# First products of 32 more expert chunks between the gate groups of a fused two-layer kernel

## The chip, the cores and the metric

The kernel runs on one core of one Trainium2 chip. The metric is the device time of one execution in microseconds. Lower is better. Before the change three timed runs gave 1766.4, 1764.07 and 1761.23 us, median 1764.07.

## The reference, cut to what matters

Two transformer layers follow each other on 256 tokens of width 1024, all in float32. The change touches two places of the first layer: the merge of its two branches, and the mixture of experts behind it.

```python
merged = sigmoid(ga) * (y_a @ w_branch_a) + sigmoid(gb) * (y_b @ w_branch_b)
h = h + merged @ w_out
n2 = rmsnorm(h, norm2_g)
# peer: 8 heads, 128 x 128 = 16384 experts, 16 chosen for each head and token
s1, s2 = scores of n2 @ wq against two sets of 128 keys
v1, i1 = top_k(s1, 16); v2, i2 = top_k(s2, 16)
vals, ci = top_k(v1[:, None] + v2[None, :], 16)     # of 256 candidates
idx = i1[ci // 16] * 128 + i2[ci % 16]; gates = softmax(vals)
h = expert_u[idx] . n2                              # the first products
out = sum(gelu(h) * gates * expert_v[idx])          # the second products
```

## The kernel before, in words

The kernel does not gather experts. It computes all 16384 of them for all 256 tokens, as 128 chunks of 128 experts, and multiplies gelu(h) by a dense gate matrix G (for each chunk, 128 experts by 256 tokens) that is zero where an expert was not chosen. Each float32 product is made of three faster ones: a weight part is split into a rounded high part (whi, written by ScalarE) and the rest (wlo, written by VectorE, or by GpSimd as bfloat16 where `pooled` says so), and so are the activations.

Weights stream from HBM in items of 1 MiB into `raw`, a ring of three slots; the SyncE queue issues them in order, each when the rest of the second part of the item three before has been written. An item is two parts of 1024 columns, one for each product of a chunk; whi and wlo are rings of three parts (`NBUF`).

The stages around the change, in order on TensorE:

1. Merge. `wide_panel` makes pa and pb (the two branch products, four banks each). VectorE multiplies them by the gates (L1707), GpSimd adds the two branches (L581), TensorE transposes the sum (L648), ScalarE and VectorE write it as high and low parts (L1195, L1591), and the output projection follows.
2. Queries and choice. TensorE computes queries and scores of 8 heads. VectorE picks the 16 best of each head (L1725 to L1748) and works out indices and gates (L1755 to L1780). Beside it TensorE computes the first products of the first `EARLY` = 24 chunks with `u_part` (24 matmuls of 256 columns; L659), ScalarE writes gelu(h) into G (L1255), and GpSimd writes the wlo of these parts (L491), up to part S_PRE - 1.
3. Gates. When `sel_ready` is set, indices and gates are transposed, and G is built in 32 groups of 8 tokens. For a group VectorE writes two one-hot matrices (L1803, 6 and 8 tokens) and two scaled ones (L1813), ScalarE scales six (L1284), TensorE multiplies them (`gate_products`, L904; 8 products, 16 records), ScalarE copies the gates of the chunks from EARLY on into G (`gate_copy`, L1291), and VectorE multiplies the gates into the first EARLY chunks, which hold gelu(h) already (`gate_times`, L1797). One-hots live in idle ring buffers, two groups deep.
4. Second products of the early chunks (`output`, `v_part`: 12 matmuls of 512 columns; L659), with one part of weights for each chunk.
5. The other 104 chunks: for each, `u_wide` (8 matmuls of 512 and 8 of 256 columns; L694, L696) two chunks ahead, then `v_part`. VectorE sums, multiplies by the gate and splits (L1851 to L1862).

The order of work on each engine is the order of the program text; engines meet at semaphores, and a wait holds up all that stands behind it on its engine.

Of the kernel before, what the change touches and what calls it, by code (L numbers as in the profile page):

```python
# [19 lines left out]
BY_ACT = 6  # L20
NEG = -3.0e38
# [24 lines left out]
EARLY = 24  # L46
# [69 lines left out]
def _wide(name, count):  # L116
    for _ in range(count - 1):
        _part()
    _part(main=f"{name}3")
    _use(*[(f"{name}{i}", "dve") for i in range(4)])  # L120
# [3 lines left out]
_wide("pb", 4)  # L124
# [13 lines left out]
assert _parts == S_LATE and EARLY % UN == 0 and (P - 2 - EARLY) % UN == 0  # L138
# [38 lines left out]


T_PART = {"n1": -1, "ya": S_WA - 1, "yb": S_WA + 3, "mg": S_WO - 1, "n2": S_WQ - 1, "idx": S_PRE - 1,
# [26 lines left out]
def program(nc, x, panels1, experts, ffa, panels2, ffb, cols, conv_cols, w_low, w_gate_up, w_sgu, k12, w_dt,  # L206
# [9 lines left out]
    with ctx:  # L216
# [50 lines left out]
        QP_AT = 24000  # L267
# [11 lines left out]
        QP = cut(16, T)  # L279
        MDEC, WG, ALR = cut(P), cut(512), cut(T)  # L280
# [13 lines left out]
        CAND = cut(NT, PEER_H, 256)  # L294
        PICK = cut(TOPK * NT * P // 2).bitcast(bf16).rearrange("p (j n) -> p j n", j=TOPK)
        VAL = cut(NT, 16, TOPK)
        IDF = cut(NT, 16, TOPK)
        BEST = cut(NT, P)
# [3 lines left out]
        IDX = cut(NT, 16, TOPK).bitcast(u32)  # L302
        CI = cut(NT, P).bitcast(u32)
        CIA = cut(NT, P).bitcast(u32)
        PST = cut(NT, PEER_H)
        assert cut.at <= QP_AT
# [75 lines left out]
        hot_ready, one_ready, one_scaled = sem("hot_ready"), sem("one_ready"), sem("one_scaled")  # L382
        gate_mm, gate_out, gate_mul = sem("gate_mm"), sem("gate_out"), sem("gate_mul")
# [69 lines left out]
        def half(item, h):  # L453
            return raw[:, item % RING, PART * h:PART * h + PART]
# [10 lines left out]
        def round_part(act, p):  # L465

            act.wait_ge(slot_ready[item_of(p) % RING], 16 * (item_of(p) // RING + 1))
            if p >= NBUF:
                wait_part_used(act, p - NBUF)
            act.activation(whi[:, p % NBUF, :], half(item_of(p), p % 2), ACT.Copy).then_inc(part_hi, 1)  # L470

        def pooled(p):

            return S_WQ <= p < S_PRE or S_ZZ <= p < S_WM
# [1730 lines left out]
```

## Time and profile before

| | |
|---|---|
| median of three timed runs | 1764.07 us |
| profiled execution, device time | 1760.97 us |
| its span, first to last instruction | 1759.3 us |
| mean granted TensorE clock | 0.959 |
| TensorE busy (matmul) | 1605.1 us, 91% |
| VectorE busy | 1254.6 us, 71% |
| ScalarE busy | 798.4 us, 45% |
| GpSimd busy | 145.2 us, 8% |

Busy times are sums over the whole span and say nothing of a single stage. A granted clock of 1.00 is 2.4 GHz and one of 0.50 is 1.2 GHz. Matmuls are pipelined: the record of one is longer than its share, so a run of them is measured from start to start.

### The profile page before, as it was taken

To read this page: it belongs to the slowest core of one execution; us is meant where nothing else is said; L and a number is where in the kernel's file an instruction comes from. 1 tells how busy PE (TensorE), PEld (TensorE's weight loads), DVE (VectorE), ACT (ScalarE), POOL (GpSimd) and SP (SyncE) were. 2 spreads that over 40 slices of the span, in tenths; PEclk is the share of its full clock that TensorE was granted. 3 is DMA by queue.
4 is the path that set the end of the run, shared out by engine and by line. 5 is a ranking of instruction groups with operands and counts; after the bars stand their busy time and mean duration, and the time that the engine had idled before them with its cause. 6 is when DMAs were issued, how large, how long until landed. Compare 5 with 4: busy or idle time off the path is not lost.

```text
span 1759.3 us, 25517 instructions
## 1 busy us (share of the span) xinstructions
PE 1605.1 (91%) x8766; PEld 1361.4 (77%) x8766; DVE 1254.6 (71%) x2098; ACT 798.4 (45%) x1190; POOL 145.2 (8%) x86
## 2 busy tenths in 40 slices
PE   6999799857899999999999999799979886879997
PEld 5777588756778888888888888688869856568886
DVE  4575469999767777777777777677774695567776
ACT  4544345469534444444444444544443533244443
POOL 1000267600000000000000000000000062000000
PEclk9999899989999999999999999899998997889999
DMA  5534334400345555555555555455543340235552
GB/s 191 186 140 154 143 122 167 143 1 0 142 169 184 189 186 186 189 190 189 191 191 191 191 191 201 138 191 191 186 160 108 108 144 1 89 139 191 191 191 95
DMA packets 38949, 270.34 MB, mean 154 GB/s; under 512 B 4706, under 2 KB 5218, under 8 KB 6643
## 3 DMA queue, kind: packets, MB, share of 16 engines
q1 hardware_dynamic: 37296, 266.97, 42.6%
q10 hardware_dynamic: 1602, 2.71, 0.5%
q8 instruction: 30, 0.49, 0.1%
q14 instruction: 21, 0.16, 0.0%
HBM read 268.62 MB, written 1.05 MB: 153 GB/s over the span
## 4 chain that ended last, share of the span: by engine, by line
PE 75%; DVE 17%; ACT 3%; issue 2%; DVEq 1%; DMA 1%; POOL 0%; SPq 0%; ACTq 0%
PE ps L659 38%; PE ps L694 20%; PE ps L696 9%; PE ps L648 2%; DVE wlo L1803 2%; PE ps L693 1%; DVE arena L2047 1%; DVE wlo L491 1%; DVE arena L2028 1%; DVE arena L1748 1%; PE ps L766 1%; DVE arena L1728 1%; DVE arena L1731 1%; DVE arena L1737 1%; ACT whi L470 1%
## 5 line engine op out<-in xcount | busy, mean ns | idle before, releaser
L694 PE MATMUL ps<-XT,whi 128*128 128x512 f32 x1536 | 554.1, 399 | 1.9 <-DVE wlo L491 1.9
L696 PE MATMUL ps<-XT,wlo 128*128 128x256 f32 x1344 | 378.6, 282 | 0.0
L694 PEld LDWEIGHTS ps<-XT,whi 128*128 128x128 f32 x1536 | 287.5, 189 | 60.6 <-DVE wlo L491 2.2
L470 ACT ACTIVATE whi<-raw 128x1024 fp32r<-128x1024 f32 x170 | 178.9, 1058 | 229.5 <-PE ps L659 177.2
L659 PE MATMUL ps<-whi,HAh 128*128 128x512 f32 x688 | 270.1, 393 | 4.8 <-DVE HAl L1926 2.3
L659 PE MATMUL ps<-wlo,HAh 128*128 128x512 f32 x688 | 269.0, 391 | 0.0
L659 PE MATMUL ps<-whi,HAl 128*128 128x512 f32 x688 | 268.3, 390 | 0.0
L696 PEld LDWEIGHTS ps<-XT,wlo 128*128 128x128 f32 x1344 | 255.6, 190 | 7.5
L491 DVE TENSOR_TENSOR wlo<-raw,whi 128x1024 fp32r<-128x1024 f32 x134 | 162.8, 1223 | 116.7 <-ACT whi L470 115.3
L1875 DVE TENSOR_TENSOR wlo<-raw,whi 128x1024 fp32r<-128x1024 f32 x192 | 232.5, 1221 | 2.0
L659 PE MATMUL ps<-XT,whi 128*128 128x256 f32 x1024 | 193.1, 314 | 4.8 <-DVE wlo L491 4.8
L1372 ACT ACTIVATE whi<-raw 128x1024 fp32r<-128x1024 f32 x108 | 114.6, 1061 | 175.3 <-PE ps L694 114.3
L659 PE MATMUL ps<-whi,XT 128*128 128x512 f32 x576 | 183.4, 406 | 11.4 <-DVE wlo L491 4.4
L1943 DVE TENSOR_TENSOR wlo<-raw,whi 128x1024 fp32r<-128x1024 f32 x108 | 132.2, 1224 | 70.7 <-ACT whi L1372 69.5
L1327 ACT ACTIVATE whi<-raw 128x1024 fp32r<-128x1024 f32 x96 | 101.9, 1061 | 165.0 <-PE ps L694 165.0
L659 PEld LDWEIGHTS ps<-XT,whi 128*128 128x128 f32 x1024 | 165.4, 201 | 6.4 <-issue 4.6
L1325 ACT ACTIVATE whi<-raw 128x1024 fp32r<-128x1024 f32 x96 | 102.1, 1064 | 134.8 <-PE ps L659 134.8
L659 PEld LDWEIGHTS ps<-wlo,HAh 128*128 128x128 f32 x688 | 129.5, 188 | 28.6
L659 PEld LDWEIGHTS ps<-whi,HAh 128*128 128x128 f32 x688 | 130.0, 189 | 27.6 <-issue 6.1
L659 PEld LDWEIGHTS ps<-whi,HAl 128*128 128x128 f32 x688 | 129.7, 188 | 28.0
L491 POOL TENSOR_TENSOR arena<-raw,whi 128x1024 bf16<-128x1024 f32 x48 | 116.4, 2427 | 371.1 <-ACT whi L470 364.8
L659 PEld LDWEIGHTS ps<-whi,XT 128*128 128x128 f32 x576 | 108.6, 191 | 34.8 <-DVE wlo L491 5.9
(264 smaller groups left out, 1985.7 us busy)
## 6 DMA issues: line engine op xcount, KB each, us to landing
raw<-in_experts SPq DMA_DIRECT2D x128, 1024.0 KB, 4.8
raw<-in_panels SPq DMA_DIRECT2D x58, 1024.0 KB, 4.8
raw<-in_ffa SPq DMA_DIRECT2D x33, 1024.0 KB, 4.8
raw<-in_ffb SPq DMA_DIRECT2D x33, 1024.0 KB, 4.8
arena<-in_row_post ACTq DMA_DIRECT2D x3, 512.0 KB, 3.7
X<-in_x SPq DMA_DIRECT2D x2, 512.0 KB, 5.7
out<-X SPq DMA_DIRECT2D x2, 512.0 KB, 2.7
arena<-in_row_ln ACTq DMA_DIRECT2D x2, 256.0 KB, 7.8
```

What stands on the lines that cost most here:

```text
L470: act.activation(whi[:, p % NBUF, :], half(item_of(p), p % 2), ACT.Copy).then_inc(part_hi, 1)
L491: eng.tensor_tensor(low_weights(p), half(item_of(p), p % 2), whi[:, p % NBUF, :].bitcast(f32), ALU.subtract).then_inc(part_lo, 1)
L648: last = pe.transpose(t_bank(stage, j)[:, P * q:P * q + P], s, ident[:, :])
L659: last = pe.matmul(out, x if w_moving else w, w if w_moving else x, start=start and n == 0, stop=stop and n == 2)
L694: last = pe.matmul(out, wh[:, k], XT[:, k], start=k == 0, stop=k == NK - 1)
L696: pe.matmul(out[:, T:], wl[:, k], XTh[:, k], start=False, stop=False)
L1325: act.activation(whi[:, p % NBUF, :], half(item_of(p), 0), ACT.Copy).then_inc(part_hi, 1)
L1327: act.activation(whi[:, (p + 1) % NBUF, :], half(item_of(p), 1), ACT.Copy).then_inc(part_hi, 1)
L1372: act.activation(whi[:, q % NBUF, :], half(item_of(q), q % 2), ACT.Copy)\
L1803: return dve.tensor_tensor(out, iota.bitcast(f32).unsqueeze(1).broadcast_to(shape), idx[:, bass.ds(g * ONES, n)].unsqueeze(2).broadcast_to ...
L1875: dve.tensor_tensor(wlo[:, (p + j) % NBUF, :], half(item_of(p), j), whi[:, (p + j) % NBUF, :].bitcast(f32), ALU.subtract).then_inc(part_lo, 1)
L1943: dve.tensor_tensor(wlo[:, q % NBUF, :], half(item_of(q), q % 2), whi[:, q % NBUF, :].bitcast(f32), ALU.subtract).then_inc(part_lo, 1)
```

## The change

`EARLY` becomes `FIRST + BESIDE` = 28 + 32 = 60. The first products of 28 chunks stand where those of 24 stood. Those of 32 more are computed between the gate groups, one chunk with `u_part` ahead of each group's products. For each group ScalarE also applies gelu to this chunk in PSUM and rounds the next weight part; VectorE also writes the rest of a weight part, multiplies the gates of 60 chunks instead of 24 and then multiplies gelu(h) into the chunk's slot of G (`beside_times`). GpSimd sets these 32 slots to 1.0 beforehand, in one memset. While groups run, raw, whi and wlo are rings of two; the third slot of each holds the one-hots. 60 chunks then go through stage 4, and 68 are left for stage 5.

In the merge, pb is finished in the order of column halves, VectorE makes the four additions that GpSimd made, and the transposes of the first half wait for the first two of them only. The tail of the choice on VectorE also changes its order: the copy of iota and the rest of part S_G stand ahead of the softmax instead of behind it. GpSimd writes the rests up to part S_G - 1, four more than before.

```diff
-EARLY = 24
+FIRST, BESIDE = 28, 32
+EARLY = FIRST + BESIDE
+S_G = S_EXP + FIRST
...
+BY_HALF = (0, 2, 1, 3)
 _wide("pa", 4)
-_wide("pb", 4)
+_wide("pb", 4, BY_HALF)
...
+I_G, I_PRE = EXP0 + FIRST // 2, EXP0 + EARLY // 2
+def ring_of(n, turn, two, three):
+    if n < two:
+        return n % turn
+    if n < three:
+        return (two + (n - two) % 2) % turn
+    return (two + (n - three)) % turn
+PART_BUF = [ring_of(p, NBUF, S_G, S_PRE) for p in range(S_END)]
+ITEM_SLOT = [ring_of(i, RING, I_G, I_PRE) for i in range(ITEMS)]
+SPARE_BUF, SPARE_SLOT = (S_G + 2) % NBUF, (I_G + 2) % RING
...
-        ones_item = EXP0 + EARLY // 2 + 2
-        ones_slot = ones_item % RING
-        b1 = (S_PRE + 1) % NBUF
-        ONE1 = whi[:, b1:b1 + 2].rearrange("p b (j c) -> p b j c", j=ONES)
-        HOT2 = wlo[:, b1:b1 + 2].rearrange("p b (j c) -> p b j c", j=ONES)
-        ONE2 = raw[:, ones_slot].rearrange("p (b j c) -> p b j c", b=2, j=ONES)
+        ONE1 = [t[:, SPARE_BUF].rearrange("p (j c) -> p j c", j=ONES) for t in (whi, wlo)]
+        ONE2 = raw[:, SPARE_SLOT].rearrange("p (b j c) -> p b j c", b=2, j=ONES)
...
-            return S_WQ <= p < S_PRE or S_ZZ <= p < S_WM
+            return S_WQ <= p < S_G or S_ZZ <= p < S_WM
...
-            stream(EXP0, EARLY // 2, experts, S_EXP)
-            stream(EXP0 + EARLY // 2, P - EARLY // 2, experts[EARLY // 2:], S_PRE)
+            stream(EXP0, FIRST // 2, experts, S_EXP)
+            beside = experts[FIRST // 2:]
+            for j in range(2):
+                load(I_G + j, beside[j])
+            with sp.Fori(0, BESIDE // 4 - 1, 1) as i:
+                for s in range(2):
+                    slot = ITEM_SLOT[I_G + s]
+                    sp.wait_ge(part_lo, i * 4 + (S_G + 2 * s + 2))
+                    sp.dma_start(raw[:, slot, :], beside[i * 2 + (2 + s)]).then_inc(slot_ready[slot], 16)
+            stream(I_PRE, P - EARLY // 2, experts[EARLY // 2:], S_PRE)
...
-            for i in range(4):
-                tt, c = i // 2, slice(512 * (i % 2), 512 * (i % 2) + 512)
-                read_out(pool, f"pb{i}")
-                pool.tensor_tensor(XN[:, tt, c], GA[:, tt, c], GB[:, tt, c], ALU.add).then_inc(merged, 1)
+            pool.wait_ge(merged, 4)
+            pool.memset(G[:, FIRST:EARLY, :], 1.0).then_inc(beside_ones, 1)
             pool.wait_ge(part_lo, S_WQ)
-            for p in range(S_WQ, S_PRE):
+            for p in range(S_WQ, S_G):
...
-            wide_panel(pb, S_WB, range(4, 8))
-            pe.wait_ge(merged, 4)
-            transposes("mg", tiles(XN, NK))
+            wide_panel(pb, S_WB, range(4, 8), order=BY_HALF)
+            transposes("mg", tiles(XN, NK), by_half=merged)
...
-                                     ONE1[:, b, j, :].bitcast(f32), ONE2[:, b, j, :], start=True, stop=True)
+                                     ONE1[b][:, j, :].bitcast(f32), ONE2[:, b, j, :], start=True, stop=True)
                 last.then_inc(gate_mm, 1)
-            pe.wait_ge(gelu_done, EARLY)
-            for g in range(2):
+            def beside(g, s):
+                pe.wait_ge(part_lo, g + (S_G + 1))
+                pe.wait_ge(beside_done, g - 1)
+                u_part(ps[:, s % 2, 0:T], S_G + s).then_inc(h_done, 1)
                 pe.wait_ge(one_ready, g + 1)
                 pe.wait_ge(one_scaled, g + 1)
-                gate_products(g)
-            with pe.Fori(1, T // (2 * ONES), 1) as pair:
-                g = pair * 2
-                for b in range(2):
-                    pe.wait_ge(one_ready, g + (b + 1))
-                    pe.wait_ge(one_scaled, g + (b + 1))
-                    pe.wait_ge(gate_out, g + (b - 1))
-                    pe.wait_ge(gate_mul, g + (b - 1))
-                    gate_products(b)
+                pe.wait_ge(gate_out, g - 1)
+                pe.wait_ge(gate_mul, g - 1)
+                gate_products(s % 2)
+            pe.wait_ge(gelu_done, FIRST)
+            for g in range(FOUR):
+                if g < 2:
+                    pe.wait_ge(part_lo, S_G + g + 1)
+                    u_part(ps[:, g, 0:T], S_G + g).then_inc(h_done, 1)
+                    pe.wait_ge(one_ready, g + 1)
+                    pe.wait_ge(one_scaled, g + 1)
+                    gate_products(g)
+                else:
+                    beside(g, g)
+            with pe.Fori(1, BESIDE // FOUR, 1) as i:
+                for s in range(FOUR):
+                    beside(i * FOUR + s, s)
             pe.wait_ge(gate_out, T // ONES)
             pe.wait_ge(gate_mul, T // ONES)
+            pe.wait_ge(beside_done, BESIDE)
...
+            def beside_gelu(g, b):
+                act.wait_ge(h_done, g + (FIRST + 1))
+                act.activation(ps[:, b, 0:T], ps[:, b, 0:T], ACT.Gelu_apprx_tanh).then_inc(gelu_done, 1)
             gate_scale(0, 0)
-            gate_scale(1, 1)
-            gate_copy(0, 0)
-            with act.Fori(1, T // (2 * ONES), 1) as pair:
-                g = pair * 2
-                for b in range(2):
-                    gate_scale(g + b, b)
-                    gate_copy(g + (b - 1), 1 - b)
-            gate_copy(T // ONES - 1, 1)
+            split_to(S_G + 1)
+            for g in range(1, FOUR):
+                beside_gelu(g - 1, (g - 1) % 2)
+                split_to(S_G + g + 1)
+                gate_copy(g - 1, (g - 1) % 2)
+                gate_scale(g, g % 2)
+            with act.Fori(1, BESIDE // FOUR, 1) as i:
+                for s in range(FOUR):
+                    g, p = i * FOUR + s, S_G + s + 1
+                    beside_gelu(g - 1, (s - 1) % 2)
+                    wait_loaded(act, item_of(p), i * 16)
+                    act.wait_ge(h_done, g + FIRST)
+                    act.activation(whi[:, buf(p), :], half(item_of(p), p % 2), ACT.Copy).then_inc(part_hi, 1)
+                    gate_copy(g - 1, (s - 1) % 2)
+                    gate_scale(g, s % 2)
+            parts[0] = S_PRE + 1
+            beside_gelu(BESIDE - 1, 1)
+            gate_copy(BESIDE - 1, 1)
...
-                for i in range(4):
+                for i in range(4) if name == "pa" else BY_HALF:
                     tt, hf = i // 2, i % 2
                     b = take(f"{name}{i}")
                     g = gate[:, tt, 512 * hf:512 * hf + 512]
                     if i == 0:
                         after("ga11" if name == "pa" else "gb11")
                     read_done(dve.tensor_tensor(g, g, b, ALU.mult))
+                    if name == "pb" and tt == 1:
+                        after(f"pb{i}")
+                        for t in range(NT):
+                            c = slice(512 * hf, 512 * hf + 512)
+                            dve.tensor_tensor(XN[:, t, c], GA[:, t, c], GB[:, t, c], ALU.add).then_inc(merged, 1)
...
+            dve.wait_ge(pool_const, 1)
+            dve.tensor_copy(iota, IOTA)
+            dve.wait_ge(part_lo, S_G)
+            split_to(S_G)
...
-            dve.wait_ge(gelu_done, EARLY)
-            split_to(S_PRE)
             turned_pair("idx", 0)
...
+            def beside_times(g, b, m):
+                dve.wait_ge(gelu_done, g + (FIRST + 1))
+                dve.wait_ge(gate_mul, g + 1)
+                slot = G[:, FIRST + m, :] if isinstance(m, int) else G[:, bass.ds(m + FIRST, 1), :].squeeze(1)
+                dve.tensor_tensor(slot, slot, ps[:, b, 0:T], ALU.mult).then_inc(beside_done, 1)
...
+                hots(ONE2[:, b, 0:BY_ACT, :], i2T, g, BY_ACT).then_inc(hot_ready, 1)
+                hots(ONE1[b], i1T, g, ONES)
                 if not first:
-                    gate_times(g + (-2), b)
+                    dve.wait_ge(beside_done, g - 1)
+                    gate_times(g - 1, 1 - b)
                 for j in range(BY_ACT, ONES):
...
+            dve.wait_ge(beside_ones, 1)
+            for g in range(FOUR):
+                split_to(S_G + g)
+                if g >= 2:
+                    dve.wait_ge(gate_mm, g - 1)
+                one_hots(g, g % 2, first=g == 0)
+                if g:
+                    beside_times(g - 1, (g - 1) % 2, g - 1)
+            with dve.Fori(1, BESIDE // FOUR, 1) as i:
+                for s in range(FOUR):
+                    g, p = i * FOUR + s, S_G + s
+                    dve.wait_ge(part_hi, g + (S_G + 1))
+                    dve.tensor_tensor(wlo[:, buf(p), :], half(item_of(p), p % 2), whi[:, buf(p), :].bitcast(f32),
+                                      ALU.subtract).then_inc(part_lo, 1)
+                    dve.wait_ge(gate_mm, g - 1)
+                    one_hots(g, s % 2)
+                    beside_times(g - 1, (s - 1) % 2, g - 1)
+            parts[0] = S_PRE
+            split_to(S_PRE)
+            dve.wait_ge(beside_done, BESIDE - 1)
+            gate_times(BESIDE - 1, 1)
+            beside_times(BESIDE - 1, 1, BESIDE - 1)
             dve.wait_ge(gate_mul, T // ONES)
+            dve.wait_ge(beside_done, BESIDE)
```

## Rows read from the trace of the kernel before

**Rows 1.** Windows by stage: busy time of each engine (x instructions), clock, DMA.

```profile
...
333.00:364.50 31.50, 14.94 (x118) 12.79 (x116) 30.77 (x58) 9.07 (x18) 7.61 (x4) 0.74 0.14 51
364.50:456.50 92.00, 66.55 (x513) 61.58 (x513) 87.26 (x159) 83.23 (x220) 0.00 (x0) 0.98 0.01 3
...
536.00:1102.70 566.70, 566.63 (x2853) 479.77 (x2854) 427.81 (x616) 247.95 (x307) 0.00 (x0) 1.00 0.54 190
...
```

**Rows 2.** Chain that ended last, at the merge: start us, us, what.

```profile
...
179.90 0.69 DVE arena L1707
...
180.66 4.94 POOL arena L581 x4
...
185.65 1.13 PE ps L648 x4
...
187.56 0.76 DVE XT L1591 x2
...
```

**Rows 3.** The same chain through the end of the choice.

```profile
...
339.11 7.66 DVE arena L1770 x16
...
349.70 5.46 DVE arena L1770 x16
...
359.31 1.13 PE ps L648 x4
...
```

**Rows 4.** Timeline of GpSimd: start us, us, instruction, idle before and releaser.

```profile
...
336.32 2.40 POOL L491 TENSOR_TENSOR arena<-raw,whi 128x1024 bf16<-128x1024 f32 x1 [0.28 <-ACT whi L470]
339.20 2.57 POOL L491 TENSOR_TENSOR arena<-raw,whi 128x1024 bf16<-128x1024 f32 x1 [0.48 <-ACT whi L470]
...
```

**Rows 5.** Timeline from the end of the choice into the gate groups, all engines.

```profile
...
359.17 1.22 DVE L491 TENSOR_TENSOR wlo<-raw,whi 128x1024 fp32r<-128x1024 f32 x1
...
364.58 5.83 PE L904 MATMUL ps<-raw,whi 128*128 128x128 f32 x32 [3.73 <-ACT raw L1284]
...
376.85 0.95 DVE L1803 TENSOR_TENSOR wlo<-HAl,sel 128x768 fp32r<-128x768 f32 x1
...
377.38 2.02 PE L904 MATMUL ps<-raw,whi 128*128 128x128 f32 x16 [1.01 <-ACT raw L1284]
377.72 1.21 DVE L1803 TENSOR_TENSOR whi<-HAl,sel 128x1024 fp32r<-128x1024 f32 x1
377.94 1.86 ACT L1284 ACTIVATE raw<-wlo,sel 128x128 f32<-128x128 f32 x6 [0.17 <-DVE wlo L1803]
378.86 0.34 DVE L1797 TENSOR_TENSOR arena<-arena,ps 128x192 f32 x1
379.12 0.59 DVE L1813 TENSOR_SCALAR raw<-HAl,sel 128x128 f32<-128x128 f32 x2
379.63 0.95 DVE L1803 TENSOR_TENSOR wlo<-HAl,sel 128x768 fp32r<-128x768 f32 x1
...
```

**Rows 6.** The chain again, early second products and the loop of the other chunks.

```profile
...
519.77 3.85 PE ps L659 x17
...
541.91 2.74 PE ps L659 x12
...
1091.69 2.74 PE ps L659 x12
...
```

**Rows 7.** Timeline of ScalarE and TensorE from the last gate group to stage 4.

```profile
...
454.28 0.86 ACT L1291 ACTIVATE arena<-ps 128x832 f32<-128x832 f32 x1 [1.41 <-PE ps L904]
...
455.04 1.99 ACT L470 ACTIVATE whi<-raw 128x1024 fp32r<-128x1024 f32 x2
...
456.46 0.47 PE L659 MATMUL ps<-whi,HAh 128*128 128x512 f32 x1 [2.22 <-DVE HAl L1834]
...
```

**Rows 8.** Groups by line, form and engine: count, busy us, mean ns, idle before.

```profile
...
L1307 ACT ACT_TABLE_LOAD x1 | 1.3, 1283 | 0.0
...
L556 POOL MEMSET arena<- 32x256 f32 x1 | 0.3, 301 | 0.0
...
```

**Rows 9.** The page's DMA issues: engine, count, KB each, us to landing.

```profile
...
raw<-in_experts SPq DMA_DIRECT2D x128, 1024.0 KB, 4.8
...
```

More of the change, by code:

```diff
@@ L113, with _wide @@
 assert _parts == S_WA
-def _wide(name, count):
+def _wide(name, count, order=range(4)):
     for _ in range(count - 1):
@@ L119, in _wide @@
     _part(main=f"{name}3")
-    _use(*[(f"{name}{i}", "dve") for i in range(4)])
+    _use(*[(f"{name}{i}", "dve") for i in order])
+BY_HALF = (0, 2, 1, 3)
 _wide("pa", 4)
-_wide("pb", 4)
+_wide("pb", 4, BY_HALF)
 _by_token("ho0", "ho1", "dve")
@@ L453, in half, with buf, wait_loaded @@
         def half(item, h):
-            return raw[:, item % RING, PART * h:PART * h + PART]
+            return raw[:, ITEM_SLOT[item], PART * h:PART * h + PART]
+        def buf(p):
+            return PART_BUF[p]
+        def wait_loaded(eng, item, more=0):
+            nth = ITEM_SLOT[:item + 1].count(ITEM_SLOT[item])
+            eng.wait_ge(slot_ready[ITEM_SLOT[item]], more + 16 * nth)
         def wait_part_used(eng, p):
@@ L512, in load @@
             def load(item, src):
-                if item >= RING:
-                    wait_item_used(item - RING)
-                sp.dma_start(raw[:, item % RING, :], src).then_inc(slot_ready[item % RING], 16)
+                before = before_in(ITEM_SLOT, item)
+                if before is not None:
+                    wait_item_used(before)
+                sp.dma_start(raw[:, ITEM_SLOT[item], :], src).then_inc(slot_ready[ITEM_SLOT[item]], 16)
             for j in range(EXP0):
@@ L639, in _, with transposes @@
         def _(pe):
-            def transposes(stage, srcs, norm=None):
+            def transposes(stage, srcs, norm=None, by_half=None):
                 for j in range((len(srcs) + 3) // 4):
                     t_claim(pe, stage, j)
+                    if by_half is not None and j % 2 == 0:
+                        pe.wait_ge(by_half, j + 2)
                     four = list(enumerate(srcs[4 * j:4 * j + 4]))
@@ L697, in u_wide, with v_part @@
                 return last
[L699 removed]
+            def v_part(outs, p, acts, start, stop, order=range(4)):
                 last = []
[L702 to L707 removed]
+                for i in order:
+                    tt, hf = i // 2, i % 2
+                    t, c = slice(P * tt, P * tt + P), slice(512 * hf, 512 * hf + 512)
+                    last.append(products(outs[i], tuple(a[:, t] for a in acts),
+                                         (whi[:, buf(p), c], wlo[:, buf(p), c]), True, start, stop))
                 return last
@@ L711, in hidden_acts, with wide_panel @@
                 return HAh[:, b], HAl[:, b], HAh[:, b]
-            def wide_panel(names, p, chunks, start=True):
+            def wide_panel(names, p, chunks, start=True, order=range(4)):
                 for n, k in enumerate(chunks):
@@ L719, in wide_panel @@
                     last = v_part([bank(name) for name in names], p + n, (XTh[:, k], XTl[:, k], XTh[:, k]),
-                                  start and n == 0, stop)
+                                  start and n == 0, stop, order)
                     if stop:
@@ L895, in _ @@
                     hidden(S_EXP + s, s % 2)
+            for n in range(FIRST // UN * UN, FIRST):
+                pe.wait_ge(part_lo, S_EXP + n + 1)
+                pe.wait_ge(gelu_done, n - 1)
+                hidden(S_EXP + n, n % 2)
             pe.wait_ge(sel_ready, 1)
@@ L1815, in one_hots @@
                 ins.then_inc(one_ready, 1)
-            for g in range(2):
-                one_hots(g, g, first=True)
-            with dve.Fori(1, T // (2 * ONES), 1) as pair:
-                g = pair * 2
-                for b in range(2):
-                    dve.wait_ge(gate_mm, g + (b - 1))
-                    one_hots(g + b, b)
-            for b in range(2):
-                gate_times(T // ONES - 2 + b, b)
+            dve.wait_ge(beside_ones, 1)
[20 more added lines that the diff above has]
+            beside_times(BESIDE - 1, 1, BESIDE - 1)
             dve.wait_ge(gate_mul, T // ONES)
+            dve.wait_ge(beside_done, BESIDE)
             def early_hidden(n, b, wait_used=True):
```

122 lines of the change are left out of this document (59 added, 63 removed).

## The prediction

> **What bounds the kernel now.** I read the windows by stage first. From 536 to 1103 us TensorE is busy 566.6 of 566.7 us at the full clock: the 104 late chunks are bound by TensorE alone. Through the gate groups (364.5 to 456.5) it is busy 66.6 of 92.0 us, VectorE 87.3 and ScalarE 83.2, with next to no DMA; ahead of them, from 333 to 364.5, TensorE is busy 14.9 of 31.5 us and VectorE 30.8 [rows 1]. So there are two holes on TensorE, one beside the choice and one in the groups, and the change puts first products into both. The chain of waits then tells who sets the end of each hole: GpSimd's four additions at the merge [rows 2], and VectorE's picking from 339 to 359 [rows 3]. The timeline shows one gate group: VectorE's first one-hots start at 376.85 and again at 379.63, 2.78 us apart with nothing idle between, against 2.02 us of TensorE products [rows 5]. VectorE sets the pace there.
>
> **The change part by part.** The sum is made on the profiled execution: 1760.97 us (span 1759.3), which lies 3.1 us under the median of 1764.07; I shift the result by this.
>
> *Chunks that leave the late loop.* A late chunk takes (1091.69 - 541.91) / 99 = 5.553 us [rows 6]. An early chunk takes, for its second products, 12 matmuls at 3.85 / 17, that is 2.718 us [rows 6]. 36 chunks move: 36 x (5.553 - 2.718) = 102.1 us less. All of it is on the path, as TensorE has no idle time in either stage. The stream asks 1 MiB in 5.44 us in stage 4, as before the change, and one lands in 4.8 us [rows 9].
>
> *Four of them beside the choice.* The first products of a chunk run at 2.88 us: GpSimd's rests, which follow them, start at 336.32 and 339.20 [rows 4]. Four more are 11.5 us, and fit into the hole in front of 359.3. But GpSimd writes their rests. VectorE's 16 picks take 5.46 us when GpSimd is idle and 7.66 us when one GpSimd rest (339.20, 2.57 us) lies at their start [rows 3, 4]: one rest holds up VectorE by 2.2 us. The four new rests fall at about 342 to 353, where VectorE picks without a pause and is the path: 4 x 2.2 = 8.8 us more. Ends: 0, if they slip into other work, and 4 x 2.57 = 10.3. I take 8.8, since these very instructions are the ones the row shows held up.
>
> *Tail of the choice.* One rest on VectorE (1.22 us [rows 5]) and the copy of iota move ahead of the softmax, where nothing hides them; before they ran beside the transposes: 1.4 us more (ends 0 and 1.6).
>
> *Merge.* Before, VectorE starts the pb products at 179.90, GpSimd adds from 180.66 for 4.94 us, the transposes start at 185.65, and VectorE's first low part at 187.56 [rows 2]. Now VectorE does two products (0.6 us from start to start of the record of 0.69) and two additions of the same size, so the transposes can start near 182.5; then two products and two additions more, up to 184.9, ahead of the low part. The low part decides: 2.7 us less (ends 0 and 3.2). The memset of 8192 columns follows on GpSimd: at 0.30 us for 256 columns [rows 8] at most 9.6 us, done before GpSimd's next work. If it held up VectorE as a rest does, that would fall on rests for which TensorE has parts in store; I take 0, with up to 6 us as the far end. The Trainium skill, SBUF — State Buffer, "Who interferes with whom", says that a VectorE instruction with two SBUF inputs contends with a GpSimd instruction that reads SBUF and not with one that only writes; the trace has no memset beside such work, so no row here shows it, and by it this end would be 0 as well.
>
> *The gate groups.* The question is the period of a group. TensorE: 2.88 for the first products plus the gate products. Their record of 16 is 2.02 us [rows 5], which includes the tail of the last one, so 4.74 to 4.90. VectorE: rest 1.22, one-hots 0.95 and 1.21, scaled 0.59 [rows 5]. `gate_times` grows from 192 to 480 elements and `beside_times` has 256; the nearest rows are 0.34 us for 192 and 0.95 for 768, so between them 0.64 and 0.41. That is 5.02 by records, but consecutive records overlap by about 0.08 (0.95, 1.21, 0.34 and 0.59 make 3.09 and fill 2.78), so about 4.6. ScalarE: scaling 1.86 [rows 5], rounding 1.0 (half of 1.99 [rows 7]), the copy of 68 chunks instead of 104, 0.86 x 68/104 or a bit above, 0.64, and a gelu near 0.45: 3.95. So TensorE is the longest, by little.
> Does the round trip fit? After the products of group g-1 end, ScalarE copies (0.6) and scales (1.9): 2.5 us. VectorE waits for that copy, multiplies 0.6 and writes the scaled ones 0.6: 1.9 us. TensorE does the next first products meanwhile for about 2.7 us. Both fit, with 0.2 us to spare on ScalarE. Behind VectorE's wait for the copy stand its scaled one-hots and the rest of the next part; this rest is ready 1.5 us before TensorE asks. With two slots, an item is asked for once in two groups, 9.6 us, against 4.8 us to land [rows 9]. I take 4.80 us for a group; ends 4.74 and 5.67 (2.88 + 2.78 with nothing side by side).
> From the first transposes (359.31) to the second products (456.46 [rows 7]) the old stage took 97.2 us. New: transposes 1.6; the first first products, cold. The granted clock of that stretch was 0.74 before, a mixture of its two levels (1.2 and 2.4 GHz) after an idle TensorE [rows 1], and the first two groups took 5.83 instead of 4.04, 1.8 us lost [rows 5]; I charge the same here: 4.7. Then 2.0 for the products, 31 x 4.80 = 148.8, 0.5 for one table load of ScalarE that is partly covered, and the tail: 2.22 before [rows 7], less 0.2 for the shorter copy, plus 0.3 and 0.4 on VectorE, 2.7. Sum 160.3: 63.1 us more.
>
> *Sum.* -102.1 + 8.8 + 1.4 - 2.7 + 63.1 = -31.5 us. The profiled execution comes to 1729.5, the median to 1732.6.
>
> **The rivals.**
> A. VectorE sets the pace. Its 4.6 us rest on the overlap of records; with three more waits in a group the overlap may be gone, and register work ahead of the short instructions may show. Then a group takes 5.02 to 5.3, say 5.2: 31 x 0.4 = 12.4 more, 1745. For it: VectorE was the pacemaker before. Against: the old group has two waits and fills 2.78 us without a gap.
> B. Better than forecast: the four rests of GpSimd cost nothing (VectorE's longer instructions keep GpSimd waiting instead), and a group takes 4.74. 8.8 + 1.9 less: 1722. Against: at 339 it was VectorE that waited.
> C. The slower side: ScalarE changes its table between gelu and scaled copy. Before, the groups had no gelu. A load takes 1.28 us [rows 8]; two in each group lift ScalarE from 3.95 to 6.5 us, past TensorE, and a group to 6.5: 31 x 1.7 = 52.7 more, 1785. The change loses from a period of 4.80 + 31.5/31 = 5.82 us on. Against: line 1307's gelu loads once for 104 chunks although roundings (a copy as well) stand between [rows 8].
> The Trainium skill, ScalarE: Activation LUTs, "Table sets: the hidden batching unit", says that copy is in every set, which the single load agrees with; "What ACT_TABLE_LOAD costs" puts a switch at about 2.66 us with its drain, by which this rival would cost 9.3 us a group, about 1872. The trace shows only the load itself, 1283 ns.
> D. The two works don't overlap: the scaled one-hots come only after the next first products, because gelu and rounding stand ahead of the copy on ScalarE and run late. 5.67 us a group: 27 more, 1760, no change.
>
> **How the numbers follow.** Chances: forecast 0.46 (own range 1724 to 1741), A 0.20, B 0.13, D 0.08, C 0.10, anything else 0.03. The range reaches over A and B, with the low end at the bounds of the unknown terms: 1718 to 1755. About 0.3%, 5.3 us, is what a measurement of this kernel can tell from no change. Faster by more: forecast, A, B and a little, 0.80. Within: D, 0.09. Slower by more: C and the like, 0.11.
>
> **What would show it.** In the changed kernel's profile: a group period of 4.8 us with TensorE nearly without idle time; TensorE at the full clock through the groups; the stage from the first transposes to the second products near 160 us; a late loop still at 5.55 us a chunk, 36 chunks shorter; the picks of VectorE between 339 and 365 with four records above 2 us; `sel_ready` some 7.5 us later than before (-2.7 + 8.8 + 1.4); the transposes of the merge 3 us earlier. The prediction is wrong if the groups take over 5.3 us, if ScalarE shows table loads inside them, if TensorE waits for a weight part there (two slots too few), or if the late chunks or the early second products change their pace.

## The result, and the profile after

The changed kernel takes 1724.40 us (median of 4 runs, 1723.58 to 1726.08) against 1762.91 for the kernel before beside it (1761.23 to 1766.40): ratio 0.9779, 95% interval 0.9765 to 0.9792, 38.5 us less. 1732.6 was forecast. The profiled execution took 1724.87 us, its span is 1723.1 us, against 1760.97 and 1759.3 before. So the two spans differ by 36.2 us, and the terms below are made on them.

The window of the gate groups in the changed kernel, with the columns of [rows 1]:

```profile
386.00:525.60 139.60, 136.66 (x1175) 136.49 (x1174) 136.45 (x209) 110.16 (x265) 0.00 (x0) 1.00 0.33 117
```

The hole of [rows 1] is filled: TensorE is busy 98% of the gate groups, where it was busy 72% before. But VectorE is busy 98% as well, so busy shares alone don't say who sets the pace. The chain of waits does. In one stretch it alternates between TensorE's first products (L704) and gate products (L951), and no other engine stands between them:

```profile
372.31 3.52 PE ps L704 x24
...
375.95 2.02 PE ps L951 x16
...
443.45 2.87 PE ps L704 x24
446.32 1.79 PE ps L951 x16
448.11 2.87 PE ps L704 x24
...
520.86 1.80 PE ps L951 x16
...
525.60 163.48 PE ps L704 x720
...
707.35 2.74 PE ps L704 x12
...
1057.21 2.74 PE ps L704 x12
...
1070.64 2.40 DVE X L1989 x4
```

One group is 2.87 + 1.79 = 4.66 us from 443.45 to 448.11. From the first gate products (375.95) to the last (520.86) it is 144.91 / 31 = 4.675 us on average, as the first two groups take 4.90 us each. The second products of the 60 early chunks are one piece of 720 matmuls, 163.48 / 60 = 2.725 us a chunk, and the late loop goes at (1057.21 - 707.35) / 63 = 5.553 us, both as in [rows 6].

The choice, on VectorE's timeline, and GpSimd's on the same stretch (line 528 of GpSimd writes a rest; L1846 of VectorE picks):

```profile
340.49 16.46 DVE L1846 SCALAR_TENSOR_TENSOR arena<-arena 128x256 bf16<-128x256 f32 x16
...
359.88 5.45 DVE L1846 SCALAR_TENSOR_TENSOR arena<-arena 128x256 bf16<-128x256 f32 x16
```

```profile
340.58 2.57 POOL L528 TENSOR_TENSOR arena<-raw,whi 128x1024 bf16<-128x1024 f32 x1 [0.48 <-ACT whi L507]
...
352.10 2.54 POOL L528 TENSOR_TENSOR arena<-raw,whi 128x1024 bf16<-128x1024 f32 x1 [0.34 <-ACT whi L507]
```

The first 16 picks take 16.46 us with five of GpSimd's rests inside, one every 2.88 us from 340.58 to 352.10; they took 7.66 with one, and the second 16 still take the 5.46 of an undisturbed row [rows 3, 4]. That is 11.0 / 5 = 2.2 us for each rest.

The chain at the merge, with the start of this stage in it:

```profile
121.17 10.03 PE ps L704 x36
...
171.33 10.08 PE ps L704 x36
...
183.72 1.29 DVE arena L1778 x2
...
191.54 8.62 PE ps L704 x35
```

GpSimd is off the chain at the merge, and the projection follows the first pb product after 7.82 us. But all of this starts 3.8 us later than before, though nothing ahead of it was changed. The same 36 matmuls in the kernel before:

```profile
120.59 8.50 PE ps L659 x36
...
169.16 8.43 PE ps L659 x36
```

The two pieces took 1.53 and 1.65 us more, and over 120.0 to 131.2 and 168.0 to 183.7 the granted clock is 0.85 and 0.89 where it was 1.00.

The account, from span to span:

| term | forecast | measured | from |
|---|---|---|---|
| up to the pb products | 0 | +3.8 | 179.90 to 183.72; 3.2 of it the two pieces above |
| merge: pb products to first output projection | -2.7 | -2.6 | 10.44 (179.90 to 190.34) to 7.82 (183.72 to 191.54) |
| choice: rests of GpSimd | +8.8 | +8.8 | 7.66 to 16.46 |
| choice: its tail | +1.4 | +1.3 | second picks to transposes 9.61 (349.70 to 359.31) to 10.88 (359.88 to 370.76) |
| choice: elsewhere | 0 | +0.2 | what is left of pb to transposes, 179.41 to 187.04 |
| gate stage | +63.1 | +57.7 | 97.15 to 154.84 (370.76 to 525.60) |
| second products and late loop | -102.1 | -103.6 | 648.66 to 545.04 (525.60 to 1070.64) |
| behind it, same instructions | 0 | -1.7 | 654.18 to 652.46; between 652.0 and 654.9 in the profiles of the changed kernel and its variants, so this says nothing of the change |
| sum | -31.5 | -36.2 | the spans (the terms are rounded) |

### The profile page after: what moved, and what is told of

Its sections match the earlier page's. It is cut to its first block, busy times and chain, and to the rows that moved or that the text cites. A ratio compares the mean times of both kernels' runs of the same rounds, so it can differ in the third digit from the quotient of the medians.

```text
span 1723.1 us, 25945 instructions
## 1 busy us (share of the span) xinstructions
PE 1596.7 (93%) x9052; PEld 1370.1 (80%) x9054; DVE 1245.9 (72%) x2058; ACT 789.1 (46%) x1190; POOL 156.9 (9%) x87
## 4 chain that ended last, share of the span: by engine, by line
PE 78%; DVE 16%; ACT 3%; issue 1%; DMA 1%; DVEq 0%; SPq 0%; ACTq 0%
PE ps L704 44%; PE ps L739 17%; PE ps L741 7%; PE ps L951 3%; PE ps L693 2%; DVE arena L1846 1%; DVE arena L2145 1%; DVE wlo L528 1%; PE ps L738 1%; DVE arena L2126 1%; DVE arena L1824 1%; PE ps L810 1%; DVE arena L1804 1%; DVE arena L1807 1%; DVE arena L1813 1%
## 5 line engine op out<-in xcount | busy, mean ns | idle before, releaser
L739 PE MATMUL ps<-XT,whi 128*128 128x512 f32 x1248 | 448.8, 399 | 1.9 <-DVE wlo L528 1.9
L741 PE MATMUL ps<-XT,wlo 128*128 128x256 f32 x1092 | 307.6, 282 | 0.0
L704 PE MATMUL ps<-XT,whi 128*128 128x256 f32 x1600 | 300.7, 306 | 4.8 <-DVE wlo L528 4.8
L507 ACT ACTIVATE whi<-raw 128x1024 fp32r<-128x1024 f32 x178 | 187.2, 1057 | 232.9 <-PE ps L704 180.1
L704 PE MATMUL ps<-whi,HAh 128*128 128x512 f32 x688 | 269.1, 391 | 5.5 <-DVE HAl L1932 2.9
L739 PEld LDWEIGHTS ps<-XT,whi 128*128 128x128 f32 x1248 | 233.0, 189 | 49.3 <-DVE wlo L528 2.2
L704 PE MATMUL ps<-wlo,HAh 128*128 128x512 f32 x688 | 268.1, 390 | 0.0
L704 PE MATMUL ps<-whi,HAl 128*128 128x512 f32 x688 | 267.7, 389 | 0.0
L704 PEld LDWEIGHTS ps<-XT,whi 128*128 128x128 f32 x1600 | 255.1, 198 | 6.4 <-issue 4.7
L528 DVE TENSOR_TENSOR wlo<-raw,whi 128x1024 fp32r<-128x1024 f32 x138 | 167.7, 1223 | 119.7 <-ACT whi L507 118.4
L741 PEld LDWEIGHTS ps<-XT,wlo 128*128 128x128 f32 x1092 | 207.7, 190 | 6.1
L704 PE MATMUL ps<-whi,XT 128*128 128x512 f32 x576 | 185.9, 411 | 11.4 <-DVE wlo L528 4.4
L1443 ACT ACTIVATE whi<-raw 128x1024 fp32r<-128x1024 f32 x108 | 114.6, 1061 | 175.3 <-PE ps L739 114.3
L2041 DVE TENSOR_TENSOR wlo<-raw,whi 128x1024 fp32r<-128x1024 f32 x108 | 132.2, 1224 | 69.5 <-ACT whi L1443 69.5
L528 POOL TENSOR_TENSOR arena<-raw,whi 128x1024 bf16<-128x1024 f32 x52 | 126.8, 2438 | 362.1 <-ACT whi L507 356.0
L704 PEld LDWEIGHTS ps<-whi,HAh 128*128 128x128 f32 x688 | 129.4, 188 | 29.3 <-issue 6.8
L704 PEld LDWEIGHTS ps<-wlo,HAh 128*128 128x128 f32 x688 | 129.2, 188 | 28.0
L704 PEld LDWEIGHTS ps<-whi,HAl 128*128 128x128 f32 x688 | 129.3, 188 | 27.7
L1973 DVE TENSOR_TENSOR wlo<-raw,whi 128x1024 fp32r<-128x1024 f32 x120 | 145.4, 1221 | 1.2
L704 PEld LDWEIGHTS ps<-whi,XT 128*128 128x128 f32 x576 | 110.1, 194 | 35.3 <-DVE wlo L528 5.9
L704 PE MATMUL ps<-XT,wlo 128*128 128x256 f32 x448 | 129.1, 288 | 0.0
L693 PE MATMUL ps<-ident,arena 128*128 128x128 f32 x184 | 41.1, 386 | 93.2 <-DVE arena L1612 42.0
```

Source lines behind the costliest of these rows:

```text
L507: act.activation(whi[:, buf(p), :], half(item_of(p), p % 2), ACT.Copy).then_inc(part_hi, 1)
L528: eng.tensor_tensor(low_weights(p), half(item_of(p), p % 2), whi[:, buf(p), :].bitcast(f32), ALU.subtract).then_inc(part_lo, 1)
L693: last = pe.transpose(t_bank(stage, j)[:, P * q:P * q + P], s, ident[:, :])
L704: last = pe.matmul(out, x if w_moving else w, w if w_moving else x, start=start and n == 0, stop=stop and n == 2)
L739: last = pe.matmul(out, wh[:, k], XT[:, k], start=k == 0, stop=k == NK - 1)
L741: pe.matmul(out[:, T:], wl[:, k], XTh[:, k], start=False, stop=False)
```

## The experiments

The kernels of this section were timed five times each, but for the last one, and beside them the kernel before took 1763.4 to 1763.6 us. Experiments 3, 7 and 8 ran beside the changed kernel itself (experiment 4); the others are compared with it by way of the kernel before.

**1. 22 first chunks in place of 28.** No rest of GpSimd falls on the picks then. Two slots of G that GpSimd presets (22 and 23) lie where the queries are written later, so they hold other values in this kernel; the number and shape of the instructions are those of 22 first chunks.

```diff
-FIRST, BESIDE = 28, 32
+FIRST, BESIDE = 22, 32
```

> The changed kernel with FIRST = 22 instead of 28: six chunks fewer are computed beside the choice, and go through the late loop. Theory (each GpSimd rest beside the picks holds up VectorE by 2.2 us, and VectorE is the path there): the six chunks cost 6 x 2.835 = 17.0 us, six rests fewer give back 6 x 2.2 = 13.2 us, so 3.8 us more than the changed kernel's 1724.4: 1728. The 16 picks that took 16.46 us take 5.5 to 7.7. Rival (the chunks beside the choice are nearly free, and the slow picks have another cause): 17 us more, 1741, and the picks stay slow.

Measured: 1732.58 us (1732.08 to 1732.95), ratio 0.9826 [0.9812, 0.9839]. The chain through the choice and at the second products:

```profile
336.87 5.47 DVE arena L1846 x16
...
345.27 5.47 DVE arena L1846 x16
...
356.15 1.54 PE ps L693 x6
...
511.83 149.99 PE ps L704 x648
...
1076.34 2.40 DVE X L1989 x4
```

Both rows of picks take 5.47. From the pb products (182.26) to the transposes it is 173.9 us against 187.04: 13.1 less, and six rests at 2.2 us are 13.2. So the hold-up is caused by the rests, and its price holds. Only five of the six rests lay beside the picks. The sixth held up a short conversion ahead of them, an instruction with a single input. VectorE's timeline has it in the changed kernel first, then in this one, where the instruction two lines above it still has a rest beside it:

```profile
337.82 2.43 DVE L1838 CAST arena<-arena 128x256 f32<-128x256 uint32 x1
```

```profile
333.63 2.48 DVE L1836 TENSOR_SCALAR arena<-arena 128x256 uint32<-128x256 uint32 x1
...
336.35 0.29 DVE L1838 CAST arena<-arena 128x256 f32<-128x256 uint32 x1
```

Six late chunks more cost 564.5 - 545.0 = 19.5 us from the second products to 1076.34, where 6 x 2.835 = 17.0 was due. A start of the second products at the lower clock (149.99 us for 54 chunks, not 147.1) explains these 2.5 us. The total lies 4 to 5 us over the theory's number, and under the rival's: the rest of that is 2.1 us behind the mixture and 0.8 us in the first first products of the gate groups (4.33 us, not 3.52), less a merge that starts 1.5 us earlier. The six chunks were worth having even with their hold-up: 17.0 us gained, 13.2 paid.

**2, 3 and 4. GpSimd's merge put back, twice, and the changed kernel again.**

```diff
-BY_HALF = (0, 2, 1, 3)
+BY_HALF = (0, 1, 2, 3)
...
+            for i in range(4):
...
+                pool.tensor_tensor(XN[:, tt, c], GA[:, tt, c], GB[:, tt, c], ALU.add).then_inc(merged, 1)
```

(TensorE waits for all four additions again; VectorE's four leave.)

> The changed kernel with the merge as it was before the change: GpSimd makes the four additions, in the old order of the quarters, and the transposes wait for all four. Theory (the merge on VectorE by halves gives 2.6 us, on the path): 1727.0. Rival (what is gained there is lost in a later wait): 1724.4, no difference.

> The changed kernel with GpSimd's merge once more, beside the changed kernel itself. From the first product of the merge to the output projection its profile took 10.5 us against 7.8 us in the changed kernel, but the medians were the same (1724.57 and 1724.4). Theory (the 2.6 us are real and were hidden by stretches at the lower clock that come by chance): side by side it is 2 to 3 us slower. Rival (what the merge gives is given back by where the idle gaps fall, and so how long the clock is low): no difference again.

> The changed kernel once more, unaltered, on the same chip as the three beside it. Its profile had two stretches of TensorE work ahead of the merge that took 10.0 us where the kernel before took 8.5, at a granted clock below 1. Theory (these are chance of one execution): the profile now shows other such stretches, and the median stays at 1724.4 within 1.5 us. Rival (they belong to this kernel): the same two stretches again.

Measured: 1724.57 us (1723.02 to 1728.24, ratio 0.9784 [0.9767, 0.9801]) the first time, 1728.66 (1726.32 to 1729.40, 0.9806 [0.9793, 0.9820]) the second, beside which the changed kernel took 1725.14 (1720.91 to 1725.53, 0.9780 [0.9766, 0.9794]). The chain of the first and of the second profile with GpSimd's merge, and of the changed kernel again:

```profile
120.97 8.46 PE ps L708 x36
...
169.52 8.46 PE ps L708 x36
...
181.06 4.94 POOL arena L627 x4
...
190.80 4.26 PE ps L708 x15
```

```profile
121.87 10.06 PE ps L708 x36
...
172.04 8.44 PE ps L708 x36
...
183.56 4.94 POOL arena L627 x4
...
193.30 1.87 PE ps L708 x6
```

```profile
121.12 10.07 PE ps L704 x36
...
171.30 10.05 PE ps L704 x36
...
183.67 1.29 DVE arena L1778 x2
...
191.48 3.70 PE ps L704 x13
```

At its own place the merge is worth what was forecast: from 0.7 us ahead of GpSimd's additions to the projection it is 10.5 us with them (180.3 to 190.80), and 7.8 on VectorE (183.67 to 191.48). In the whole time it is 3.5 us in the pair that ran side by side, and 0.2 us in the first run, where the rival of that expectation had the right number. What blurs it are the pieces at 121 and 171: each is about 8.45 or about 10.05 us long. One execution with GpSimd's merge has no long one, the other has one, both of the changed kernel have two. So the expectation of the third run, other pieces in a second profile, was not met. But the pieces don't belong to the kernel's instructions: the kernels with 22 first chunks and with 5 scalings on ScalarE (below) have the same instructions as the changed one up to there, and their profiles have one long piece and none. And executions of one kernel do differ: the changed kernel took 1720.91 us once, at a mean granted clock of 0.964, and 1724.96 to 1725.53 in the other four, at 0.961 or 0.962. The rival of the second run, that the merge itself shifts how long the clock is low, stays open: the median clock was 0.963 and 0.960 in the two runs with GpSimd's merge.

**5 and 6. Who sets the group's period: one scaled one-hot more, or less, on ScalarE.**

```diff
-BY_ACT = 6
+BY_ACT = 7
```

and 5 in the other kernel. ScalarE writes 7 of the 8 scaled one-hots of a group, or 5; VectorE the others.

> The changed kernel with BY_ACT = 7 instead of 6: of the 8 scaled one-hots of a group ScalarE scales 7. VectorE has 0.13 us less in a group (0.26 less for a scaled one, 0.13 more for the one-hots), ScalarE 0.31 more. Theory (TensorE sets the pace of 4.66 us with 2.87 + 1.78): no difference, 1724.4. Rival (VectorE sets it): 32 x 0.13 = 4 us less, 1720. If ScalarE's round trip of copy and scaling were the limit, 10 us more, 1734.

> The changed kernel with BY_ACT = 5: VectorE has 0.13 us more in a group, ScalarE 0.31 less. VectorE's work in a group fills 4.62 of 4.66 us in the trace. Theory (TensorE sets the pace and VectorE is 0.04 behind it): a group takes 4.75, 3 us more, 1727.5. Rival (VectorE has real slack behind the overlap of records): 1724.4.

Measured: 7: 1735.65 us (1730.66 to 1736.01), ratio 0.9830 [0.9812, 0.9848]. 5: 1724.76 us (1724.08 to 1725.57), ratio 0.9782 [0.9768, 0.9796]. The timeline of the changed kernel over one group (L951 gate products, L704 first products, L1349 copy of the gates, L1342 scalings; in brackets the idle time before and its releaser):

```profile
450.82 1.95 PE L951 MATMUL ps<-raw,whi 128*128 128x128 f32 x16
...
452.52 0.48 PE L704 MATMUL ps<-XT,whi 128*128 128x256 f32 x2
...
452.89 0.62 ACT L1349 ACTIVATE arena<-ps 128x544 f32 x1 [0.55 <-PE ps L951]
453.41 1.86 ACT L1342 ACTIVATE raw<-raw,sel 128x128 f32<-128x128 f32 x6
...
455.47 1.73 PE L951 MATMUL ps<-raw,wlo 128*128 128x128 f32 x14
```

With 7, ScalarE's timeline, TensorE's timeline, and from the chain the products of the group before:

```profile
453.15 0.62 ACT L1349 ACTIVATE arena<-ps 128x544 f32 x1 [0.84 <-PE ps L951]
453.67 2.15 ACT L1342 ACTIVATE raw<-raw,sel 128x128 f32<-128x128 f32 x7
```

```profile
455.92 2.02 PE L951 MATMUL ps<-raw,whi 128*128 128x128 f32 x16
457.69 0.48 PE L704 MATMUL ps<-XT,whi 128*128 128x256 f32 x2
```

```profile
450.97 2.02 PE ps L951 x16
```

With 6 the scalings end at 455.27 and the first gate product starts at 455.47, 0.20 us later. (The chain has this piece start at 455.64, since it counts a piece from the end of the record before; the 1.79 and 2.02 us of its pieces are cut differently for that reason and can't be compared.) With 7 the scalings end at 455.82 and the product starts 0.10 us later, and so it is in nearly all groups of both profiles: 0.17 to 0.22 us against 0.09 to 0.11. So the round trip (gate products, copy of the gates, scalings, next gate products) becomes the limit, and a group takes 4.91 to 4.95 us, 4.92 on average (the one shown 4.95). The spare time was 0.20 - 0.10 = 0.10 us, half the 0.2 that I had named in the prediction. One scaling more is 0.29 us, of which 0.19 has no cover, and from the first gate product to the next first product it is 1.78 us and not 1.70, 0.08 more: together 0.27, and the period grew by 0.26. Here my own expectation, no change, was wrong although the number that would have told it was on record; its last branch, ScalarE's round trip as the limit and 1734 us, is what came. VectorE's relief (it now waits for ScalarE's copy, 6.5 us in all from 400 to 500) brought nothing. With 5, VectorE has one scaling more and a shorter row of one-hots (640 columns, not 768), is busy 100.00 of 100.00 us from 400 to 500, and the period is 4.66 to 4.69: its work has just reached TensorE's. The whole stage from the transposes to the second products is 155.5 us against 154.8. The 3 us more of the expectation did not come; the rival's number did.

**7. The last seven rests of GpSimd put on VectorE, between the picks.**

```diff
+POOL_END = S_EXP + 21
...
-            for p in range(S_WQ, S_G):
+            for p in range(S_WQ, POOL_END):
...
+            def beside_rest(us):
+                worked[0] += us
+                if worked[0] >= 1.74 and parts[0] < S_G:
+                    worked[0] = 0.0
+                    split_to(parts[0])
+
+            dve.wait_ge(part_lo, POOL_END)
+            split_to(POOL_END)
```

(`beside_rest` is called behind each pick and each piece of the sums.)

> The changed kernel, with the last seven of GpSimd's rests (chunks 21 to 27) written by VectorE instead, one about every five picks. Theory (each GpSimd rest holds up VectorE by 2.2 us there, and VectorE writes one itself in 1.14 us): 7 x (2.2 - 1.14) = 7.4 us less, 1717. The picks show no record above 0.5 us. Rival (VectorE is not held up by GpSimd, so the seven rests are work added to the path): 7 x 1.14 = 8 us more, 1732. If the fixed places of the rests make TensorE wait, it comes between the two.

Measured: 1717.72 us (1714.31 to 1718.76), ratio 0.9735 [0.9720, 0.9749]; 7.4 us less than the changed kernel beside it (1725.14). The chain:

```profile
363.79 1.44 PE L694 MATMUL ps<-ident,arena 128*128 128x128 f32 x6 [3.92 <-DVE arena L1874]
...
518.52 166.23 PE ps L705 x720
```

The transposes start at 363.79 and not at 370.76, 7.0 us earlier. A rest that VectorE writes itself has a record of 1.22 us and takes 1.14 from start to start; one of GpSimd's costs it 2.2: 7 x (2.2 - 1.14) = 7.4 was expected. The second products then give back 2.8 us, since they start at the lower clock in this profile (166.23 against 163.45 us in the changed kernel's); it is the slowest of the five executions, which lie at 1714.3 (two) and at 1717.7 to 1718.8 (three). So the hold-up is shown from both sides: take the rests away (22 first chunks) or take them to the engine that they hold up.

**8. 34 first chunks with rests on VectorE.** What was left then was TensorE's idle time ahead of the transposes (3.92 us in the line above, and more before it). Against the kernel of experiment 7:

```diff
-FIRST, BESIDE = 28, 32
+FIRST, BESIDE = 34, 32
...
-            act.wait_ge(top_shift, 1)
-            act.activation(GS, GS, ACT.Exp).then_inc(top_exp, 1)
+                if n == turned_to + 1:
+                    act.wait_ge(top_shift, 1)
+                    act.activation(GS, GS, ACT.Exp).then_inc(top_exp, 1)
...
-            split_to(S_G)
...
+            split_to(S_G)
```

(The rests that are left by then go behind the softmax.)

> As the kernel with the rests on VectorE, with FIRST = 34 (six chunks more beside the choice, 66 early in all), thirteen rests on VectorE and ScalarE's exponential of the softmax moved ahead, between the gelus of chunks 25 and 26. Theory (TensorE has nothing to do before the choice ends, so more chunks fit until TensorE itself is the path): six chunks leave the late loop, 17.0 us less; the last first product ends near 376.6, so the gate stage starts 5.9 us later than in the changed kernel; TensorE comes warm into it, 1.8 us less; the gates of 66 chunks cost VectorE 0.05 us a group, 1.6 us; the two table loads in the middle 1 us. Together 10.3 us less than 1724.4: 1714. Rival (a group is bound by VectorE so closely that its added work and the stall of the table loads eat it): as the kernel with seven rests, 1717 or above.

Measured: 1714.40 us (1712.29 to 1716.18), ratio 0.9719 [0.9706, 0.9733]. This beats both kernels: 10.7 us under the changed one, 49.0 under the one before. Against experiment 7 it is 3.3 us less, but the two intervals overlap. In the profiles the transposes start 7.8 us later than in the changed kernel (5.9 were forecast), the gate stage is 0.9 us shorter, and the second products and the late loop are 15.9 us shorter (17.0 forecast). The windows of its groups:

```profile
390.00:527.00 137.00, 137.00 (x1178) 137.00 (x1177) 136.61 (x208) 108.03 (x267) 0.00 (x0) 1.00 0.32 112
```

TensorE runs the first products from 369.99 into the transposes (378.63) without a gap, but it idled twice for about 1 us at 359 and 363, each time for a rest of VectorE (1.06 and 0.83 us): the pacing of the rests is not yet right.

**9. Gates of the first chunks only.** It takes work off VectorE and ScalarE and none off TensorE. This kernel leaves out the gates of the 32 chunks beside the groups. It was timed once.

```diff
-BY_ACT = 6
+BY_ACT = 5
...
-                early = G[:, 0:EARLY, bass.ds(g * ONES, ONES)]
+                early = G[:, 0:FIRST, bass.ds(g * ONES, ONES)]
```

> The changed kernel with BY_ACT = 5 and with the gates of the 28 first chunks only worked out in each group (the 32 chunks beside get no gate numbers: their part of the arena keeps what was there). That takes about 0.27 us a group off VectorE and 0.3 us off ScalarE against the kernel with BY_ACT 7. Theory, TensorE alone sets the group's period (2.87 us of first products and 1.79 us of gate products without a gap): the period stays 4.66 us, TensorE stays busy through 390 to 525 us, VectorE and ScalarE idle, and the time is that of the changed kernel, 1724. Rival, VectorE's or ScalarE's work of each group still sets it: the period falls to about 4.5 us or less, the gate stage is 4 to 5 us shorter, 1719 to 1720.

Measured: 1725.69 us (the kernel before beside it 1765.97). Its window and chain:

```profile
386.00:525.00 139.00, 136.73 (x1175) 136.53 (x1173) 131.86 (x237) 101.43 (x236) 0.00 (x0) 1.00 0.33 116
```

```profile
443.51 2.87 PE ps L704 x24
446.38 1.79 PE ps L951 x16
448.17 2.87 PE ps L704 x24
```

VectorE is at 131.9 us of 139 and ScalarE at 101.4, and the period stays 4.66. TensorE alone sets it; VectorE's 98% was a coincidence of sizes.

## Why the prediction was right

**Who bounds the groups: right.** TensorE does, with ScalarE's round trip 0.10 us behind and VectorE, busy 136.45 of 139.60 us, about 0.1 us. The two experiments with one scaling more or less and the one with fewer gates show it. Rival A had VectorE at 5.02 to 5.3 us: the records' overlap that it doubted is still there, and VectorE's work fits in 4.6. Rival D (5.67) fell with the period. Rival B named the better side and its number (1722) is the nearer one, but for half the wrong reason: the group was shorter, the rests were not free.

**The size of a group: 0.125 us too long.** I took 4.80, inside ends of 4.74 and 5.67, since the gate products' record of 2.02 us held the tail of the last matmul [rows 5]. That was the right reason, but the tail is larger than I allowed: from the first gate product to the next first product it is 1.70 us (450.82 to 452.52), and 1.78 with a late input, not 1.86 to 2.02. The first products then take 2.96 us and not 2.88, and the measured 4.66 lies below my lower end of 4.74. 31 x 0.125 = 3.9 us: the largest error. The rest of the stage's 5.4 us too much: the first first products took 3.52 + 0.13 us and not the 4.7 that I charged for a start at the lower clock (with 22 first chunks they took 4.33), and the table load (one, at 375.83, line 1353), for which I charged 0.5, is already in the average of 4.675: behind it the copy of the gates starts 2.40 us after the first gate product and not 2.07. The tail is 2.94 us from the last gate products to the second products, against 2.7.

**The choice: right, to 0.1 us.** A price read from one pair of rows of the kernel before (7.66 against 5.46, one rest between them) held for five. The step to keep is that it was looked for at all: four chunks "beside" an engine's work cost 8.8 of the 11.3 us (4 x 2.835) that they save.

**The late loop: right.** 36 x 2.835 = 102.1 against 103.6. The 1.5 us: before, some matmuls of the second products ran slowly at the start (seven records of 0.63 us from 457.79 on, 0.39 at full clock); in the changed kernel's profile they start at the full clock, behind 2.94 us without a matmul. This is no gain of the change that one can count on: five of the ten profiles of the changed kernel and its variants start them slowly (with 5 scalings on ScalarE they took 165.06 us, with the rests on VectorE 166.23).

**The merge: right at its place** (2.62 for 2.7), not resolved in the median. GpSimd's memset, which I bounded by 9.6 us and priced at nothing, took 6.94:

```profile
188.91 6.94 POOL L625 MEMSET arena<- 128x8192 f32 x1 [171.72 <-DVE arena L1783]
```

VectorE's rest at 193.22, inside it, took 1.22 us, the same as the one at 196.13, outside. The Trainium skill, SBUF — State Buffer, "Who interferes with whom", says that a VectorE instruction with two SBUF inputs contends with a GpSimd instruction that reads SBUF, and not with one that only writes it. This row bears out the second half, and the 16.46 us the first.

**Not in the forecast:** 3.2 us at the lower clock ahead of the merge, and 1.7 us less behind the mixture, both of a size that differs between executions. That they nearly cancel with the 1.5 us above (+3.8 against -1.5 and -1.7) is luck. The forecast was 8.2 us high: 31.5 against 36.2 on the spans is 4.7 of that, and 3.1 came from the shift to the median of the runs: the profiled execution of the changed kernel lies 0.5 us over its median, not 3.1 under it.

**Rival C, the only one on the slower side, fell** with its condition: one table load in 32 groups of gelu, copy and scaling. The Trainium skill, ScalarE: Activation LUTs, "What ACT_TABLE_LOAD costs", adds a drain of about 1.38 us to a load. Here the gelu follows at 377.1, 1.3 us from the load's start at 375.8, and the scalings before it end at 375.81, so that no idle time of the drain's size is to be seen on either side.

## What to carry to other kernels

When two stages leave different engines idle, put them side by side, and take the period from the longest engine's own work once its inputs are early, from start to start and not from a record with its tail: the round trip over the other engines only has to fit, and its spare time (here 0.10 us of 4.66) tells what a change of division will do. Price "free" work beside VectorE by what it holds up: find in the old trace two rows of the same instructions, one with and one without the other engine's work beside them. If GpSimd holds VectorE up for longer than VectorE would need itself (2.2 against 1.14 us), the work belongs on VectorE, and GpSimd should have it only where VectorE has time.

## What the runs showed of the hardware

- VectorE's scalar_tensor_tensor from two SBUF inputs stops for the most part while GpSimd's tensor_tensor runs: 16 picks of 5.46 us in all took 7.66 with one such instruction of GpSimd and 16.46 with five. Each of GpSimd's is 2.39 to 2.40 us alone and about 2.55 with the picks beside it. So the one loses 2.2 us and the other 0.15. Two inputs are not needed for this: a tensor_scalar and a cast of VectorE with one SBUF input each (128x256, 32 bits) took 2.48 and 2.43 us beside such an instruction and 0.28 to 0.29 without.
- The granted clock falls in some executions and not in others, at the same places of the program (to 0.83 on average over each of the two long pieces of the changed kernel): pieces of 36 matmuls are 8.43 to 8.50 or 10.03 to 10.09 us long, nothing between, in all eleven profiles. Of the ten of the changed kernel and its variants, eight are long at 121 us and five at 171 us, none at 157 us; the one of the kernel before has none. The second products of the early chunks likewise start slowly in five of these ten. Differences of 1.6 to 3.2 us between two kernels need several executions for that reason. What decides whether it falls was not found.
- From the first of 16 gate products to the first product of the next chunk it is 1.70 us when their inputs are there in time and 1.78 when TensorE has to wait for the last one (the first two groups, and all groups with 7 scalings on ScalarE): a late input costs 0.08 us more than its own lateness.
